# Hybrid attention encoder step: an earlier signal for the window keys, another buffer for the last tile's rows, a bulk copy of keys issued in the next phase, and other units for GpSimd

## What is computed

```
n = rms_norm(x);  qa, ka, va, qd, kd, vd = split(n @ w_in)      # 1024 -> 2304, rotary on q and k
a = sink_attention(qa, ka, va)      # 8 heads, 2 kv heads, window of 128 frames + 16 meta rows
d = diff_attention(qd, kd, vd)      # 4 heads, two softmaxes each, all earlier frames
h = x + concat(a, d) @ w_out
y = rms_norm(h + swiglu(rms_norm(h)))

def diff_attention(q, k, v, mask, lam, ...):
    p = softmax(where(mask, q @ k * scale, -inf))
    w = p[..., 0, :, :] - lam * p[..., 1, :, :]
    return rms_norm(w @ v) * ...
```

## Time and profile before

| | us |
|---|---|
| three runs | 2848.01, 2848.20, 2848.41 |
| median | 2848.2 |
| the profiled execution | 2848.2 |
| its span, first to last instruction | 2846.3 |
| PE busy in the span | 2643.3 (93%) |
| VectorE, ScalarE, GpSimd busy | 1600.8, 1124.2, 389.6 |
| projection loop | about 80 to 595 |
| last two trips and the change of phase | 595 to 653 |
| stages 0, 1, 2, 3, 4 of the differential attention | from 653, 683, 737, 836, 971 |
| output product and feed-forward | from 1189 |

### The profile page before, as it was taken

How to read it: one execution, slowest core, us unless ns; L and a number is a source line. 1 busy time by engine, 2 the same in 40 slices (tenths; PEclk the granted TensorE clock), 3 DMA queues, 4 the chain that set the end, 5 groups by cost and what they waited for, 6 DMA issues and landing times.

```text
span 2846.3 us, 47898 instructions
## 1 busy us (share of the span) xinstructions
PE 2643.3 (93%) x19784; PEld 1640.0 (58%) x19784; DVE 1600.8 (56%) x3258; ACT 1124.2 (39%) x2048; POOL 389.6 (14%) x486
## 2 busy tenths in 40 slices
PE   0899999967899999499999999999999999999998
PEld 0566666635667776255565655656565656556564
DVE  7477666646988886356535444352525354443526
ACT  2476666645888889344411201111111112011113
POOL 0111111101665546100000000000000000000001
PEclk9999999975999999799999999999999999999999
DMA  4122111132110001232201010101000010101003
GB/s 161 56 69 80 63 61 57 56 88 58 42 31 13 24 20 39 108 119 89 75 16 38 8 45 1 45 1 45 30 16 30 15 38 8 45 1 45 1 8 122
DMA packets 111739, 132.87 MB, mean 47 GB/s; under 512 B 42786, under 2 KB 88994, under 8 KB 110498
## 3 DMA queue, kind: packets, MB, share of 16 engines
q1 hardware_dynamic: 111522, 129.82, 14.2%
HBM read 92.20 MB, written 34.84 MB: 45 GB/s over the span
## 4 chain that ended last, share of the span: by engine, by line
PE 57%; DVE 1%; ACT 0%; issue 0%; DMA 0%; POOL 0%; POOLq 0%; ACTq 0%
PE y_ps L2168 6%; PE y_ps L2170 6%; PE y_ps L2169 6%; PE hnT_ps L2155 6%; PE hnT_ps L2156 6%; PE hnT_ps L2157 6%; PE mixT_ps L2155 5%; PE mixT_ps L2156 5%; PE mixT_ps L2157 5%; PE y_ps L2140 2%; PE y_ps L2141 2%; PE y_ps L2142 2%; PE mixT_ps L2117 1%; PE hnT_ps L2127 0%; DVE tail_buffers L1913 0%
## 5 line engine op out<-in xcount | busy, mean ns | idle before, releaser
L1938 DVE SCALAR_TENSOR_TENSOR residual_rows<-y_ps,pair_scales,residual_rows 128x512 f32<-128x512 f32 (+1 forms) x374 | 277.0, 748 | 101.3 <-PE y_ps L2170 100.3
L2155 PE MATMUL hnT_ps<-ffn_inT_hi,tail_buffers 128*128 128x352 f16 x1056 | 330.7, 313 | 0.7 <-ACT ffn_inT_hi L2035 0.7
L2156 PE MATMUL hnT_ps<-ffn_inT_lo,tail_buffers 128*128 128x352 f16 x1056 | 330.8, 313 | 0.0
L2157 PE MATMUL hnT_ps<-ffn_inT_hi,tail_buffers 128*128 128x352 f16 x1056 | 330.6, 313 | 0.0
L2155 PE MATMUL mixT_ps<-ffn_inT_hi,tail_buffers 128*128 128x352 f16 x1056 | 330.1, 313 | 0.0
L2157 PE MATMUL mixT_ps<-ffn_inT_hi,tail_buffers 128*128 128x352 f16 x1056 | 330.0, 313 | 0.0
L2156 PE MATMUL mixT_ps<-ffn_inT_lo,tail_buffers 128*128 128x352 f16 x1056 | 330.0, 313 | 0.0
L2064 ACT ACTIVATE w_out_halves<-mixT_ps,pair_scales 128x352 f32<-128x352 f32 x66 | 36.5, 553 | 706.2 <-PE mixT_ps L2157 706.2
L2168 PE MATMUL y_ps<-w_out_halves 128*128 128x512 f16 (+1 forms) x748 | 283.8, 379 | 0.0
L2169 PE MATMUL y_ps<-w_out_halves 128*128 128x512 f16 (+1 forms) x748 | 283.5, 379 | 0.0
L2170 PE MATMUL y_ps<-w_out_halves 128*128 128x512 f16 (+1 forms) x748 | 283.5, 379 | 0.0
(11 more groups left out here) (289 smaller groups left out, 5403.3 us busy)
## 6 DMA issues: line engine op xcount, KB each, us to landing
tail_buffers<-in_w_gate SPq DMA_DIRECT2D x11, 1024.0 KB, 5.5
tail_buffers<-in_w_up SPq DMA_DIRECT2D x11, 1024.0 KB, 8.1
tail_buffers<-in_w_down SPq DMA_DIRECT2D x22, 512.0 KB, 3.2
keys_values<-in_w_in SPq DMA_DIRECT2D x8, 1152.0 KB, 15.2
x_tile<-in_x SPq DMA_DIRECT2D x17, 512.0 KB, 3.5
tail_buffers<-mix_scratch SPq DMA_DIRECT2D x17, 512.0 KB, 3.6
residual_rows<-in_x SPq DMA_DIRECT2D x17, 512.0 KB, 4.5
out_y_prompt<-tail_buffers SPq DMA_DIRECT2D x16, 512.0 KB, 2.6
```

Of the source, the lines that this page charges most:

```text
L1938: nc.vector.scalar_tensor_tensor(out, YP[(2 * t + n) % 4][0:rows, :], PS[0:rows, i, F_YI:F_YI + 1], out, ALU.mult, ALU.add).then_inc(h_ok, 1)
L2155: nc.tensor.matmul(out, FH[w][:, k, c], nh, start=k == 0, stop=False)
L2156: nc.tensor.matmul(out, FH[w][:, k, c], nl, start=False, stop=False)
L2157: last = nc.tensor.matmul(out, FL[w][:, k, c], nh, start=False, stop=k == KC - 1)
```

## The change

Four edits:

- Two new semaphores, `kw_hi` and `kw_lo`, rise behind the second instruction of `split_hi` and `split_lo`. VectorE's first two wait for `kw_hi`, its other two for `kv_hi`. window_transposes waits for `kw_lo` instead of `kv_lo`, and so does SyncE's copy of the window values.
- The last tile's rows (j = 16) are written to the first half of X, the tile `x_tile`, that is no longer used by then, and stored from there. normalise(16, kv) waits for no store.
- The copy of tiles 4 to 14 of K2 leaves `load_diff`; the copy at the head of the next phase takes tiles 4 to 15.
- GpSimd makes the lo halves of all diag units and all packed full units in stages 1 to 4, and of three in four of the other full units of 512 columns in every stage.

```diff
+        rows_out = lambda j: AO[:, :] if j < NT else X[:, 0:HS * HD]
...
                 def store_out(j, kv):
                     sp.wait_ge(o_out, 2 * j + kv + 1)
                     c = slice(GRP * HD * kv, GRP * HD * (kv + 1))
-                    sp.dma_start(g.mix[rows(j), c], AO[:, c]).then_inc(ao_stored[kv], 16)
+                    sp.dma_start(g.mix[rows(j), c], rows_out(j)[:, c]).then_inc(ao_stored[kv], 16)
 
                 def before_values(j):
 
-                    sp.wait_ge(kv_hi, j)
-                    sp.wait_ge(kv_lo, j)
+                    sp.wait_ge(kw_hi, j)
+                    sp.wait_ge(kw_lo, j)
...
                     sp.dma_start(K2D[0:HD, :, 0:4 * P], K1[0:HD, :, 0:4 * P]).then_inc(g.k2_in[1], 16)
-                    sp.dma_start(K2D[0:HD, :, 4 * P:(NT - 1) * P], K1[0:HD, :, 4 * P:(NT - 1) * P]).then_inc(g.k2_in[2], 16)
...
                 def split_lo(j):
-                    dve.wait_ge(kv_hi, j + 1)
+                    dve.wait_ge(kw_hi, j + 1)
...
                     nc.vector.scalar_tensor_tensor(VO[j % WRING][:, 1, :, 0:HD], zh(C_VA, C_QD, HD), col(S_A),
-                                                   VO[j % WRING][:, 0, :, 0:HD], ALU.mult, ALU.subtract)
+                                                   VO[j % WRING][:, 0, :, 0:HD], ALU.mult, ALU.subtract).then_inc(kw_lo, 1)
+                    dve.wait_ge(kv_hi, j + 1)
...
                     n = 2 * j + kv
-                    if j:
+                    if 0 < j < NT:
                         dve.wait_ge(ao_stored[kv], 16 * j)
...
-                    nc.vector.tensor_tensor(AO[:, GRP * kv * HD:GRP * (kv + 1) * HD].rearrange("p (h d) -> p h d", h=GRP),
+                    nc.vector.tensor_tensor(rows_out(j)[:, GRP * kv * HD:GRP * (kv + 1) * HD].rearrange("p (h d) -> p h d", h=GRP),
...
-                    nc.scalar.activation(VO[j % WRING][:, 0, :, 0:HD], zh(C_VA, C_QD, HD), ACT.Copy, scale=col(S_A))
+                    nc.scalar.activation(VO[j % WRING][:, 0, :, 0:HD], zh(C_VA, C_QD, HD), ACT.Copy, scale=col(S_A)).then_inc(kw_hi, 1)
...
                 def window_transposes(j):
-                    pe.wait_ge(kv_lo, j + 1)
+                    pe.wait_ge(kw_lo, j + 1)
...
+                every = slice(0, P)
...
-                    pool = wide and fulls % 4 in POOL_FULL or kind == "full" and cols == 4 * P and gr.frame and gr.n < 2
+                    pool = wide and fulls % 4 in POOL_FULL or gr.frame and rows == every and len(blocks) > 1
...
-                sp.dma_start(K2[0:HD, :, (NT - 1) * P:NT * P], K1[0:HD, :, (NT - 1) * P:NT * P]).then_inc(k2_in[2], 16)
+                sp.dma_start(K2[0:HD, :, 4 * P:NT * P], K1[0:HD, :, 4 * P:NT * P]).then_inc(k2_in[2], 16)
...
-                            pe.wait_ge(k2_in[stage], (48, 16, 32)[stage])
+                            pe.wait_ge(k2_in[stage], (48, 16, 16)[stage])
```

More of the change, by code:

```diff
@@ L325, in phase_project @@
             s(n) for n in ("xT", "xT_hi_out", "xT_lo_out", "z", "rot_mul", "rot_add", "v"))
-        kv_hi, kv_lo, qh_ok, qlw_ok, qld_ok = (s(n) for n in ("kv_hi", "kv_lo", "q_hi", "wq_lo", "dq_lo"))
+        kw_hi, kw_lo, kv_hi, kv_lo, qh_ok, qlw_ok, qld_ok = (s(n) for n in ("wkv_hi", "wkv_lo", "kv_hi", "kv_lo", "q_hi", "wq_lo", "dq_lo"))
         kdt_ok, kt_out, qdt_ok, qd_out, qwt_ok, qw_out, kwt_ok, kw_out, kw2_out = (
```

## The result

The changed kernel takes 2822.6 us (median of 4 runs, 2817.7 to 2825.2), the kernel before, run beside it, 2848.3 us (2848.0 to 2852.8). The ratio is 0.9904, 95% interval [0.9887, 0.9921]: 22 to 32 us faster. The forecast was 2825.6 us, range 2818 to 2834.

The account below looks back on a forecast made before the run. PE was taken as the bound outside its holes, so an edit pays only by closing one. Terms 5.4 + 1.9 + 9.3 + 3.0 + 3.0 = 22.6 us took 2848.2 to 2825.6 us, range 2818 to 2834.

Parts of the forecast that it names:

- Split signal in the loop: Projection loop: signalling after two instructions instead of four removes all 16 PE waits for window-key transposes, -5.4 us.
- Rival (d): Projection loop: another wait takes over and the signal doesn't help; 5.4 us less gain, 2831.0 us, chance 0.04.
- Last trip: Projection's last trip: first exponentials start near 600.1 instead of 602.04, limited by ScalarE's earlier work; -1.9 us, bounds 1.4 and 2.5.
- Buffer and copy: Projection's end: last normalise waits for no store and 1408 KB leave SyncE's queue, so stores land sooner; -9.3 us (8.6 to 10.0).
- the far end of 2.0: Projection's end: if the bulk copy isn't what delays the stores, they land at 647.6 + 1.2, a gain of 2.0 us.
- Stage 1: Differential attention, n = 0: VectorE loses two diag subtractions a group to GpSimd, PE idles less; -3.0 us, ends 5.9 and 1.7.
- The 4.2 us set against it: Differential attention, n = 0: VectorE's maxima slowed while GpSimd subtracts, 1.4 us a group, 4.2 us.
- rival (b): Differential attention, n = 0 and 1: GpSimd blocks VectorE, eating the relief; 16.6 us gain left, 2831.6 us, chance 0.11.
- Stage 2: Differential attention, n = 1: fourth full unit goes to VectorE, 0.87 us at four group ends; -3.0 us, ends 4.8 and 0.
- Stages 3 and 4: Later differential attention: VectorE loses 32 subtractions, GpSimd gains them, neither is waited for; 0, ends -1 and +1.
- The clock: PE's granted clock of 0.50 or 1.00: rise and dip may move either way; 0, ends -3 and +3 us.
- Rival (c): Slower than before: low clock stays through differential attention's n = 0 stretch, +27 us, 2853.0 us, chance 0.03.

Follow-up runs that it names:

- the first trace: First profiled execution of the changed kernel with all four edits, the fastest of its four: 2817.7 us.
- the kernel with half of the signal: Kernel before, with PE signalled after two of VectorE's four instructions but VectorE starting them when it did before: 2839.7 us, ratio 0.9970.
- The 40 in the idle stretch alone: Changed kernel plus 40 unread products of 384 columns on PE between the projection's last product and the phase change: 2824.8 us, ratio 0.9919.

## Why the prediction was right

The time came 3.0 us below the forecast, inside the range, by the mechanisms that it named. Term by term:

- **Split signal in the loop, forecast 5.4, measured 7.4** (8.2 in the first trace, with an early start of 0.8). Mechanism right, size off. The step that failed took the wait shown in rows 2 for the whole hole; it shows 0.31 of 0.47 us a tile. The row alone couldn't tell it; the period of the tile could only after the change. Rival (d) falls.
- **Last trip, forecast 1.9 (1.4 to 2.5), measured 1.5.** The bound of ScalarE's finish was the right idea. PE's second hole of 1.28 us, for ScalarE's copies of the tile before, is the part that the working didn't price.
- **Buffer and copy, forecast 9.3 (8.6 to 10.0), measured 11.4.** Beyond even the far end of 10.5. Two steps were too small. SyncE's arrival at the stores was held at 637.89 on the old scale; without the bulk copy its issues take less time (3.65 us from the copy of 512 KB to the first store, 6.23 before). And the landings then take 3.5 us, with which the last one comes at 630. The order of the two edits was right: the copy is what counts (7.0 us), the buffer alone is near nothing (1.9), as the far end of 2.0 had it.
- **Stage 1, forecast 3.0 (1.7 to 5.9), measured 1.0.** The step that failed priced the relief of VectorE against PE's idle time in total, without asking in each wait what stood ahead of the maxima. The 4.2 us set against it didn't come either: L1417 kept its 184 ns in stage 1 (186 in rows 7), as GpSimd was idle at all four of them, and L1421 its 162. So L1417 was no sign of rival (b) in this stage; what stretched was the meta subtraction.
- **Stage 2, forecast 3.0 (0 to 4.8), measured 3.7.** Size near, reason half right: the working gave the fourth unit 0.87 us at each of four ends. PE's waits there went from 6.4 to 4.5 us only, as the third end got longer (1.97 us, before 1.59), behind GpSimd's diag unit. The rest came from the diag units that left VectorE, to which the forecast gave nothing. That the sum of the two was near 3.0 is luck.
- **Stages 3 and 4, forecast 0, measured 0.** VectorE lost 32 subtractions there and PE's wait for ScalarE stayed 5.9 us.
- **The clock, forecast 0 +-3.** Its ends were too near: stage 1's first group alone decides over 3.9 us by chance, more than the term's bound. In the median it came out near 0. The dip in stage 2, priced at 1.7 us, is worth about 1.0: the third group takes 25.4 us before, and 24.4 in the kernel with half of the signal, whose dip lies elsewhere. Rival (c) didn't come.

The loop, the phase change and stage 2 gave 2.0, 2.1 and 0.7 us more than forecast, stage 1 and the last trip 2.0 and 0.4 less. The errors cancel by half: the terms as measured add to 25.0 us, against 22.6 forecast and 25.7 by the medians. With stage 1 at its measured 1.0 us the forecast would have been 20.6 us, 5.1 below the measured change, so part of its nearness is luck.

## What to carry to other kernels

Take a short wait of PE in a row as a lower bound of the hole (0.31 shown, 0.47 gained here) and judge it by the loop's period, and price the relief of an engine wait by wait: look at what stands directly ahead of the instruction that ends each wait. When a store is late, look at what is ahead of it in the queue before giving it another buffer, and count the issuing engine's own stalls. Where a phase change leaves PE at the low clock and the next stage doesn't fill it, a few dozen unread products that hold the clock can cost less than the low clock does. The 40 in the idle stretch alone bought nothing here; with more in the stage behind it the gain came.

## What the runs showed of the hardware

The granted clock of 0.50 can outlast long stretches of busy PE: 24.7 of 28.1 us busy and then 13.7 of 14.3, without a rise, and in other executions of the same kernel the rise comes at the end of the first of these. Stage 0 at 1.00 instead of 0.50 gained 3.5 us of 28 only, and VectorE is busy 20.9 of 24.6 us there, which I take for the reason. SyncE's issue of the same transfer takes 0.62 or 0.43 us in the changed kernel and 2.20 or 2.65 us behind 1408 and 512 KB that are on their way.
